# Index heads, keys and dots turned inside the panels q0 and q1, last keys inside v1, on one core

## What is computed

```python
proj = h @ w_in                      # q, k, v: 16 heads x 64; qi: 8 index heads x 64; ki: 64; wi: 8
q = rope(rmsnorm(q)); k = rope(rmsnorm(k))
qi = rope(qi); ki = rope(rmsnorm(ki)); wi = wi * 8 ** -0.5
# for each block of 128 queries
s_idx = einsum('qhd,kd->qhk', qi, ki) * 64 ** -0.5
score = einsum('qhk,qh->qk', relu(s_idx), wi)      # causal
_, sel = top_k(score, 128)
p = softmax(q . k[sel] * 64 ** -0.5)               # 16 heads
out = (p @ v[sel]) @ w_o
```

## Time and profile before

| | us |
|---|---|
| median of 3 runs | 1995.17 (1994.8 to 1997.59) |
| profiled execution | 1996.37 |
| its span | 1994.6 |
| TensorE busy | 1909.3 |
| VectorE, ScalarE, GpSimd busy | 766.4, 749.7, 848.5 |
| q0's first matmul | 671.63 |
| v0's first matmul | 735.70 |
| v1's last transposes | 826.43 |
| w_o's first matmul | 909.33 |

### The profile page before, as it was taken

One profiled execution on the slowest core, in us unless ns is written; L12 is line 12 of the kernel. 1 busy time (PEld: TensorE's weight loads), 2 busy tenths in 40 slices (PEclk: granted clock), 3 DMA queues, 4 the chain that ended last, 5 costly groups with the idle time before them and its releaser, 6 DMA issues.

```text
span 1994.6 us, 25043 instructions
## 1 busy us (share of the span) xinstructions
PE 1909.3 (96%) x9679; PEld 1542.6 (77%) x9679; DVE 766.4 (38%) x1292; ACT 749.7 (38%) x1160; POOL 848.5 (43%) x417
## 2 busy tenths in 40 slices
PE   2899999999999999999999999999998999999998
PEld 2677888888888868667888888888775768888887
DVE  7984231111002378882311110020636556503621
ACT  5534342232223244683422221243448362212212
POOL 1002443444444558654434444444335444434443
PEclk8799999999999899899999999999999999999999
DMA  5014233333332212102333323333420313233331
GB/s 126 13 25 139 85 85 105 89 100 95 100 101 70 85 64 85 64 2 64 85 105 84 105 83 107 108 107 96 132 74 2 95 43 105 85 105 90 100 106 63
DMA packets 210348, 168.29 MB, mean 84 GB/s; under 512 B 19537, under 2 KB 175641, under 8 KB 210200
## 3 DMA queue, kind: packets, MB, share of 16 engines
q1 hardware_dynamic: 207120, 162.05, 27.7%
q10 hardware_dynamic: 3144, 5.08, 0.8%
HBM read 162.63 MB, written 2.13 MB: 83 GB/s over the span
## 4 chain that ended last, share of the span: by engine, by line
PE 87%; DVE 5%; ACT 3%; issue 2%; POOL 1%; SPq 1%; DMA 1%; POOLq 0%; DVEq 0%; ACTq 0%
PE PS L2039 75%; PE PS L2304 2%; PE PS L2295 2%; PE PS L2314 1%; PE PS L1943 1%; PE PS L1944 1%; PE PS L2103 1%; DVE taken L1829 1%; POOL w_lo L623 1%; ACT probs_t L1141 1%; PE PS L1964 1%; PE PS L1976 1%; ACT w_hi L848 0%; SPq L473 0%; ACT probs L1130 0%
## 5 line engine op out<-in xcount | busy, mean ns | idle before, releaser
L623 POOL TENSOR_TENSOR w_lo<-raw,w_hi 128x2048 fp32r<-128x2048 f32 x147 | 679.7, 4624 | 974.3 <-ACT w_hi L848 841.7
L848 ACT ACTIVATE w_hi<-raw 128x2048 fp32r<-128x2048 f32 x147 | 281.6, 1916 | 644.3 <-PE PS L2039 644.2
L2039 PE MATMUL PS<-xT_hi,w_hi 128*128 128x512 f32 (+1 forms) x1152 | 441.1, 383 | 1.5 <-DVE xT_lo L1537 1.1
L2039 PE MATMUL PS<-xT_lo,w_hi 128*128 128x512 f32 (+1 forms) x1152 | 438.2, 380 | 0.0
L2039 PE MATMUL PS<-xT_hi,w_lo 128*128 128x512 f32 (+1 forms) x1152 | 438.2, 380 | 0.0
L2039 PEld LDWEIGHTS PS<-xT_hi,w_hi 128*128 128x128 f32 x1152 | 216.6, 188 | 46.8 <-issue 6.4
L2039 PEld LDWEIGHTS PS<-xT_lo,w_hi 128*128 128x128 f32 x1152 | 216.6, 188 | 41.8
L2039 PEld LDWEIGHTS PS<-xT_hi,w_lo 128*128 128x128 f32 x1152 | 216.7, 188 | 40.5
L2039 PE MATMUL PS<-w_hi,hT_hi 128*128 128x512 f32 x608 | 236.9, 390 | 0.0
L2039 PE MATMUL PS<-w_hi,hT_lo 128*128 128x512 f32 x608 | 236.6, 389 | 0.0
L2039 PE MATMUL PS<-w_lo,hT_hi 128*128 128x512 f32 x608 | 236.6, 389 | 0.0
(11 more groups left out here) (337 smaller groups left out, 2085.5 us busy)
## 6 DMA issues: line engine op xcount, KB each, us to landing
raw<-in_ffn_w_gate_up SPq DMA_DIRECT2D x88, 512.0 KB, 4.9
raw<-in_ffn_w_down SPq DMA_DIRECT2D x40, 512.0 KB, 4.4
raw<-in_w_up SPq DMA_DIRECT2D x32, 512.0 KB, 4.8
raw<-in_w_down SPq DMA_DIRECT2D x32, 512.0 KB, 4.5
raw<-in_dsa_w_in SPq DMA_DIRECT2D x28, 512.0 KB, 4.2
raw<-in_w_in SPq DMA_DIRECT2D x21, 512.0 KB, 4.3
raw<-in_s_w_glu SPq DMA_DIRECT2D x16, 512.0 KB, 4.5
raw<-in_dsa_w_o SPq DMA_DIRECT2D x8, 512.0 KB, 4.3
```

The costliest lines, as they stand in the source:

```text
L623: pool.tensor_tensor(w_lo[:, par, :], raw[:, par, :], f32(w_hi[:, par, :]), ALU.subtract).then_inc(w_split, 1)
L848: act.activation(w_hi[:, par, :], raw[:, par, :], ACT.Copy).then_inc(w_rounded, 1)
L2039: ins = mm(o, a if weights_stay else c, c if weights_stay else a, start=first and n == 0, stop=last and n == 2)
```

## The change

It changes the order of work on four engines, and moves four additions.

- TensorE: turn_heads(0) goes to place 0 of q0, the ki transposes to place 3, the dots of block 1 to places 4 to 7 of q0, those of blocks 2 and 3 to places 0 to 4 of q1, turn_heads(1) to place 5. turn_heads(4) goes to place 2 of v1, and the dots of the first four attention units to places 4 and 5. The last pair of heads takes its blocks as 2, 3, 1, 0.
- ScalarE: index copies ahead of q0's squares, relus with them; the rounding of the second slot behind the squares of q0 and q1; all key scales of k1 and head_turned(4) ahead of slot 57; the first four exponentials between v1's copies.
- VectorE: scores of block 1 among the heads of q0, the others ahead of those of q1; block 2 is finished before the heads of k0, and 9 rounds of block 3 instead of 4 stand ahead of the heads of k1. For k1, VectorE adds the rotary parts itself.
- GpSimd: no additions for k1; the w_lo of v1's second slot behind the four reciprocal roots of k1.

```diff
-            for b in (0, 2, 1, 3):
+            for b in ((0, 2, 1, 3) if hp < NH // 2 - 1 else (2, 3, 1, 0)):
...
 POOL, in the loop over the panels
-                    if tb == 2:
+                    if tb == 2 and name != "k1":
                         split_run(g + 3, 1)
...
-                        head_add(3 * TB + n)
+                        if name == "k0":
+                            head_add(3 * TB + n)
                         key_rstd(n, panel, tb)
...
+                if name == "k1":
+                    split_run(g + 3, 1)
...
 ACT, q0
-            round_run(g + 2, 1)
-            for tb in range(TB):
-                if tb == TB - 1:
-                    round_run(g + 3, 1)
-                head_square("q0", tb)
             head_turned(0, qiT, 0)
             act.wait_ge(ki_t, 1)
             act.activation(kiT[:, :], PS[:, 0, :], ACT.Copy).then_inc(ki_t_sb, 1)
+            round_run(g + 2, 1)
+            for tb in range(TB):
+                head_square("q0", tb)
+                index_relu(2 * tb)
+                index_relu(2 * tb + 1)
+            round_run(g + 3, 1)
 ACT, q1
-            for i in range(2 * NI):
+            for i in range(NI, 3 * NI - 2):
                 index_relu(i)
             round_run(g + 2, 1)
-            for tb in range(TB):
-                if tb == TB - 1:
-                    round_run(g + 3, 1)
-                head_square("q1", tb)
-                for i in range(2):
-                    index_relu(2 * NI + 2 * tb + i)
+            index_relu(3 * NI - 2)
+            index_relu(3 * NI - 1)
+            head_square("q1", 0)
+            head_square("q1", 1)
             head_turned(1, qT, 0)
+            head_square("q1", 2)
+            head_square("q1", 3)
+            round_run(g + 3, 1)
 ACT, after k1
             head_turned(3, kT, 0)
-            key_scale(4)
-            key_scale(5)
+            for n in range(TB, 2 * TB):
+                key_scale(n)
+            head_turned(4, kT, 4)
             round_run(head_slot("v1") + 2, 1)
-            key_scale(6)
-            key_scale(7)
-            values_out("v1", 0, 4)
-            head_turned(4, kT, 4)
...
-            columns_act(dsa_units, DSA_UNIT, dsa_columns)
+            values_out("v1", 0, 2)
+            exponent(dsa_units, DSA_UNIT, 0, 8)
+            exponent(dsa_units, DSA_UNIT, 1, 8)
+            values_out("v1", 2, 3)
+            exponent(dsa_units, DSA_UNIT, 2, 8)
+            exponent(dsa_units, DSA_UNIT, 3, 8)
+            values_out("v1", 3, 4)
+            columns_act(dsa_units, DSA_UNIT, dsa_columns, ahead=2)
 DVE, in head(name, tb)
+                if name == "k1":
+                    dve.wait_ge(head_sin, n + 1)
+                    st = stage[:, 0, tb, :]
+                    tt(st, st, head_s[:, tb, :], ALU.add).then_inc(key_added, 1)
 DVE, the index part
             for tb in range(TB):
                 head("q0", tb)
-            for i in range(2 * NI):
+                index_score(2 * tb)
+                index_score(2 * tb + 1)
+            for i in range(NI, 3 * NI):
                 index_score(i)
             for tb in range(TB):
                 head("q1", tb)
-                for i in range(2):
-                    index_score(2 * NI + 2 * tb + i)
...
             choose_rounds(1, 0, ROUNDS)
             choose(1)
-            choose_rounds(2, 0, 12)
+            choose_rounds(2, 0, ROUNDS)
+            choose(2)
             for tb in range(TB):
                 head("k0", tb)
-            choose_rounds(2, 12, ROUNDS)
-            choose(2)
-            choose_rounds(3, 0, 4)
+            choose_rounds(3, 0, 9)
             for tb in range(TB):
                 head("k1", tb)
-            choose_rounds(3, 4, ROUNDS)
+            choose_rounds(3, 9, ROUNDS)
 PE
+            def index_first(place):
+
+                if place == 0:
+                    turn_heads(0)
+                if place == 3:
+                    ... the wait for ki_done and the four key transposes, as before
+                if place >= 4:
+                    index_dots((place - 4,))
+
+            def index_rest(place):
+
+                if place < 5:
+                    index_dots(((4,), (5, 6), (7, 8), (9, 10), (11,))[place])
+                if place == 5:
+                    pe.wait_ge(idx_relu, 3 * NI)
+                    turn_heads(1)
+
+            panel(head_slot("q0"), head_panel("q0"), after=index_first)
+            panel(head_slot("q1"), head_panel("q1"), after=index_rest)
...
+            def attention_ahead(place):
+
+                if place == 2:
+                    turn_heads(4)
+                if place in (4, 5):
+                    pe.wait_ge(head_t_sb, 20)
+                    for t in (2 * place - 8, 2 * place - 7):
+                        columns_dot(dsa_units, DSA_UNIT, col_max, t)
+
+            panel(head_slot("v1"), head_panel("v1"), after=attention_ahead)
+            columns_pe(dsa_units, DSA_UNIT, 3 * KT, col_max, TB * (DSA_PANEL + 9), ahead=2)
```

More of the change, by code:

```diff
@@ L317, in program @@
             sem("head_sq_done"), sem("head_sin"), sem("head_added"), sem("head_rstd"), sem("head_done"), sem("q_rstd"))
-        head_t, head_t_sb = sem("head_t"), sem("head_t_sb")
+        head_t, head_t_sb, key_added = sem("head_t"), sem("head_t_sb"), sem("key_added")
         ki_squared = sem("ki_squared")
@@ L1035, in key_scale @@
                 st = stage[:, (3 + n // TB) % 2, n % TB, :]
-                act.wait_ge(head_added, 3 * TB + n + 1)
+                if n < TB:
+                    act.wait_ge(head_added, 3 * TB + n + 1)
+                else:
+                    act.wait_ge(key_added, n - TB + 1)
                 act.wait_ge(head_rstd, n + 1)
@@ L2256, in _, with index_dots @@
             n_slot(g + 2, (g + 2) % 2, DSA_PANEL + 1, range(KT), xT_hi, xT_lo, True, True, DSA_W - 3 * D - 512)
[L2257 to L2267, removed]
+            def index_dots(dots):
+                for i in dots:
                     if i == 0:
@@ L2277, in index_dots @@
                            start=True, stop=True).then_inc(idx_dot, 1)
-            panel(head_slot("q1"), head_panel("q1"), after=index_dots)
-            pe.wait_ge(idx_relu, 3 * NI)
-            turn_heads(1)
+            def index_first(place):
+                if place == 0:
+                    turn_heads(0)
+                if place == 3:
+                    pe.wait_ge(ki_done, 2)
+                    pe.wait_ge(head_t_sb, 1)
+                    for tb in range(TB):
+                        ins = tr(PS[:, 0, P * tb:P * tb + P], ki_st[:, tb, :, :].rearrange("p a d -> p (a d)"), ident[:, :])
+                    ins.then_inc(ki_t, 1)
+                if place >= 4:
[8 more added lines that the diff above has]
+            panel(head_slot("q1"), head_panel("q1"), after=index_rest)
             panel(head_slot("v0"), head_panel("v0"))
@@ L2286, in _ @@
             turn_heads(3)
-            panel(head_slot("v1"), head_panel("v1"))
-            turn_heads(4)
             def columns_dot(units, u0, s_read, t):
@@ L2330, in columns_pe @@
                         weigh(p - 3)
-            pe.wait_ge(head_t_sb, 20)
-            columns_pe(dsa_units, DSA_UNIT, 3 * KT, col_max, TB * (DSA_PANEL + 9))
+            def attention_ahead(place):
[7 more added lines that the diff above has]
+            columns_pe(dsa_units, DSA_UNIT, 3 * KT, col_max, TB * (DSA_PANEL + 9), ahead=2)
             g, last = WO_SLOT, 3 * KT + KT
```

## The result

The changed kernel takes 2005.05 us (median of 7 runs, 2004.03 to 2007.3), the kernel before 1997.48 in 7 runs (1993.49 to 2000.43; the three shown at first are among them). The ratio is 1.0043, 95% interval 1.0032 to 1.0055: slower by 8.6 us (6.4 to 11); the medians alone differ by 7.6. I forecast slower, by 6.3. The direction is as forecast, and so is the mechanism of the wait ahead of k1; the cost of the last keys is not. The time lies 0.55 us above the forecast's own range (to 2004.5) and 0.05 us above the range over all cases (to 2005).

The account below looks back on a forecast made before the run. It took TensorE, busy 96% of the span, as the bound, so reordering moves only gaps. Terms -1.4 + 10.0 + 2.0 + 2.7 - 5.7 - 1.3 = +6.3 us on 1995.17 gave 2001.5, range 1998 to 2004.5.

Parts of the forecast that it names:

- the last keys: At turn_heads(4) in panel v1: TensorE waits for ScalarE's key scales, +2.7 us (1 to 4).
- The index part: In q0 and q1: waits go, a smaller wait on scores comes back, v0 starts 1.4 us earlier (1.0 to 3.8).
- VectorE's order and GpSimd's passes: Ahead of k1: k0's head late at V + 53.5 (V: v0's first matmul), TensorE waits 10.0 us (1.6 to 10.7).
- The clock: Behind the wait ahead of k1: granted clock falls, 2.0 us lost (1.3 to 3).
- Start of attention: From v1's last transposes to pair 7's dots: 5.7 us gained (3 to 7).
- tail: Last four blocks of the attention loop, reordered 2, 3, 1, 0: waits shrink, 1.3 us gained (0 to 2).
- A: Rival, ahead of k1: choose(1) escapes GpSimd, wait 1.6 us, clock holds; -4.1 us, 1991.1; chance 0.17.
- B: Rival, ahead of k1: choose(1) held by the first pass only, wait 4.7 us; +0.3 us, 1995.5; chance 0.17.
- C: Rival: the wait of (b) and more collisions at block 3, +4.6 us, about 2006; chance 0.06.
- (b): Ahead of k1: block 1's mask comes behind GpSimd's pass and is held, choose(1) too; k0's head at V + 54.2.

Follow-up runs that it names:

- kernel 1: Changed kernel with VectorE's order from block 2's rounds on put back to that of the kernel before; ratio 0.9999 to the kernel before, stage 237.67 us.
- kernel 2: Changed kernel with GpSimd's two w_lo passes made to wait for VectorE's mask and choose(1); ratio 1.0020 to the kernel before, stage 242.36 us.
- kernel 3: Changed kernel with the edits of kernel 1 and kernel 2 together; ratio 0.9970 to the kernel before, stage 231.51 us.
- kernel 5: Kernel before with only the change from k1 on (attention part), without VectorE's order of rounds; ratio 0.9978 to the kernel before, stage 233.55 us.
- kernel 6: Kernel before with only the last two pairs' blocks reordered to 2, 3, 1, 0; ratio 0.9994 to the kernel before, stage 235.82 us.
- kernel 4: Kernel before with only the index part of the change, inside q0 and q1; ratio 1.0009 to the kernel before, stage 240.46 us.

## Why the forecast was right on k1's wait and wrong on the last keys

- **The index part (-1.4).** Measured -2.4. The one wait left in q1 is 0.58 us, where I took 2.2: the error is in the scores' lateness, within its bounds. The 3.8 us of waits that went, less 0.58, would be 3.3; the other 0.9 us have the size of what the clock ahead of q0 moves from kernel to kernel (last section), but nothing here shows that it is that.
- **VectorE's order and GpSimd's passes (+10.0).** Measured 10.35, with k0's head at V + 53.9 where I had 53.5. Kernels 1 and 2 show the two causes apart: without the order 2.24 us, without the two collisions 4.87, without both none.
- **The clock (+2.0).** The second part grew by 13.11 us, of which 10.35 are the wait: 2.8.
- **The last keys (+2.7).** This is the step that failed, in size and in part in mechanism. Measured 4.84 us, and behind it 1.6 us lost at the half clock, under which the sixteen transposes ran, which I had put at nothing: 6.4 for 2.7. I had worked ScalarE's chain out from k1's last matmul. ScalarE's timeline, after, which answers to the earlier trace rows:

```profile
812.48 0.60 ACT L1034 ACTIVATE head_sq<-PS 128x512 f32<-128x512 f32 x1 [5.81 <-DVE head_ss L1685]
...
817.27 3.94 ACT L1046 ACTIVATE stage<-stage,head_rs 128x64 f32<-128x64 f32 x16
821.81 4.02 ACT L1046 ACTIVATE stage<-stage,head_rs 128x64 f32<-128x64 f32 x16 [0.60 <-POOL head_rs L610]
```

  It is VectorE that sets it: k1's first head began only at 810.57, so the square ahead of the rounding came 1.9 us behind k1's last matmul, and the scales paused 0.60 us for a root. In kernels 3 and 5, where VectorE is in time, the same square follows that matmul by 0.3 and 0.5 us; the waits are 3.58 and 3.79, of which 0.58 and 0.59 are the same pause. VectorE's lateness has its own collision in it: the mask of block 3 was held for 4.09 us instead of 0.28, and behind it VectorE had no gap up to k1's head. Without these 3.8 us that head would have begun near 806.8, before k1's last matmul, as in kernels 3 and 5; so 1.1 to 1.3 of the 4.84 us are, by this estimate, the price of that collision. No run isolates it.
- **Start of attention (-5.7) and tail (-1.3).** From k1's transposes to pair 7's dots (810.59 to 854.65) it is 44.06 us, against 44.33 before: what remains beside the 6.4 just named is a gain of 6.7. Kernel 5, whose clock stays up there, gives 6.3 by the same sum (its third part is 4.6 shorter in spite of a wait of 3.79, and 2.0 of that is kernel 6's order). From there to w_o 60.03 against 62.13: 2.1, of which kernel 6 puts 1.9 to the last order.
- **Sum.** Forecast -1.4 + 12.0 - 4.3 = +6.3; measured -2.4 + 13.1 - 2.4 = +8.4. The rest of the miss is the median that I started from: 1995.17 in three runs, 1997.48 in seven; without that shift of 2.3 us the time would lie inside the range, with the last keys wrong all the same. Rivals A and B are out: both of the collisions took place. C asked for the wait of (b) and more collisions at block 3. One came, at the mask and not at the scan or the adds, and TensorE paid for it ahead of turn_heads(4); the time lies 1 us from C's 2006 and 3.6 from the forecast's 2001.5.

The range's upper end was too near. I had bounds of 1 to 4 us on the last keys, which leave out that the engine feeding ScalarE would itself be late, and that the clock would fall behind this wait too.

What stays open: why the granted clock held in kernel 1 and fell in kernel 4 (below); what the changed order would cost with the mask of block 3 kept off its pass as well; and how kernel 3 would do with VectorE's rounds shortened instead of moved. The last two weren't tried.

## What to carry to other kernels

An engine with little busy time (VectorE, 39%) can set the end for a stretch: count its queue from release to deadline, with every instruction that a GpSimd pass can hold (here two-input ones, a scan and tensor_scalar, for up to 5.2 us), before putting work ahead of an instruction that frees a PSUM bank. When it is late, look for each later deadline on its queue, for the lateness is paid at all of them until it has caught up. And before judging an edit by its time, restore one edit at a time: here a part worth -4.2 us and one worth +2.8 came out as +8.4 with a reordering that cost 8.4 on top of both, and the best version keeps both parts, drops the reordering and puts two GpSimd passes behind VectorE's mask and choice.

## What the runs showed of the hardware that I had not expected

- Who is held is settled within 0.1 us, and what decides it isn't shown. In the changed kernel GpSimd's pass began 0.05 us behind the start of VectorE's scan (754.40 and 754.45): the scan kept its 0.75 us and the pass took 5.11 instead of 4.60. In kernel 4 the distance was 0.04 us (757.55 and 757.59), the pass kept 4.61 and the scan took 5.19; kernel 1 has the same distance and the same 5.19. GpSimd's roots on small tensors did not hold VectorE: in the changed kernel one ran from 759.99 for 3.07 us (2.90 for the one behind it), and the mask of block 2 at 760.55 took its 0.28. Beside these roots the traces don't show the lock of the passes.
- The clock's price has little to do with the length of the wait. What the second part lost beyond the wait ahead of k1 is 2.8 us for 10.35 us of wait, 2.4 for 4.87, 1.9 for 2.22 (kernel 4) and 0.3 for 2.24 (kernel 1). The same window behind the wait, first in kernel 1, then in kernel 4:

```profile
780.00:782.00 2.00, 2.00 (x10) 1.00 0.00 0
782.00:784.00 2.00, 2.00 (x10) 1.00 0.00 0
```

```profile
780.00:782.00 2.00, 0.73 (x3) 1.00 0.00 0
782.00:784.00 2.00, 2.00 (x6) 0.55 0.00 0
```

  Two waits of the same length, one with the fall and one without. Ahead of turn_heads(4) a longer wait came off better: 3.79 us in kernel 5 left the granted clock at 1.00, behind 3.58 in kernel 3 it was 0.50 from 813 to 815 us.
- Ahead of q0 the clock falls without any wait, at the 72-column matmuls of the small panel: in the changed kernel the granted clock is 1.00 from 650 to 655 us and 0.50 from 655 on, with TensorE busy throughout. How long the half clock reaches into q0 moves the first part by about 1 us from kernel to kernel (83.3 to 84.6 in those with the same index part), which is noise under every comparison of stages here.
